# Four more matrix products of a long fp32 kernel by 7 block products in place of 8, with the modulation chunks moved to other stages

## The reference

```python
def conv_ffn(h, w_in, conv_w, conv_b, w_out):
    a = dwconv3(h @ w_in, conv_w, conv_b)
    gate, up = jnp.split(a, 2, axis=-1)
    return (jax.nn.silu(gate) * up) @ w_out
...
    q, k, v, u, g = jnp.split(h_lat @ w_in, splits, axis=-1)      # first mixer
...
    y_lat = jnp.concatenate([a_lat, s_lat], axis=-1) @ w_out      # first mixer
...
    kc = (hc @ w_k).reshape(nb, nl, N_ATTN_HEADS, 2, ATTN_DH)     # differential attention
    k = apply_rope_2(k.reshape(nb, ns, N_ATTN_HEADS, 2, ATTN_DH), cos, sin)
...
    mod = jax.nn.silu(c) @ w_ada[li] + b_ada[li]                  # modulation, all layers
    sh1, sc1, gt1, sh2, sc2, gt2 = jnp.split(mod[:, None, :], 6, axis=-1)
...
    g_a, g_s = jnp.split(jax.nn.sigmoid(gates), 2, axis=-1)
    return (g_a * ya + g_s * ys) @ w_out
```

## Time and profile before

| what | value |
|---|---|
| time, median of 3 runs | 4127.28 us (4125.02 to 4127.33) |
| time of the profiled execution | 4124.42 us |
| its span, first to last instruction | 4122.6 us |
| TensorE busy | 3827.7 us, 93% of the span |
| mean granted TensorE clock | 0.963 of full speed |
| DVE, POOL, ACT busy | 1544.5, 1021.0, 848.5 us |
| DMA traffic | 568.18 MB, mean 138 GB/s |

### The profile page before, as it was taken

One profiled execution on the slowest core, in us unless ns is written; L12 is line 12 of the kernel. 1 busy time (PEld: TensorE's weight loads), 2 busy tenths in 40 slices (PEclk: granted clock), 3 DMA queues, 4 the chain that ended last, 5 costly groups with the idle time before them and its releaser, 6 DMA issues. The chain is left out here.

```text
span 4122.6 us, 40757 instructions
## 1 busy us (share of the span) xinstructions
PE 3827.7 (93%) x14868; PEld 2394.7 (58%) x14868; DVE 1544.5 (37%) x2529; ACT 848.5 (21%) x1794; POOL 1021.0 (25%) x1357
## 2 busy tenths in 40 slices
PE   7998999999999998998989999999989979999994
PEld 3545765555685547667864755756568764444442
DVE  2015465650153334236650434555463351111115
ACT  1106310000031111021010423543420221111111
POOL 0006132210001022104420013300033215555555
PEclk9999999999999999999999999989999979999996
DMA  6610011125311111431222214721112219999995
GB/s 239 223 68 9 31 41 61 61 73 193 137 53 63 36 46 49 152 134 61 92 88 80 77 41 189 311 72 36 41 57 82 71 70 363 390 394 393 378 358 198
DMA packets 132615, 568.18 MB, mean 138 GB/s; under 512 B 20974, under 2 KB 27118, under 8 KB 115840
## 3 DMA queue, kind: packets, MB, share of 16 engines
q0 software_dynamic: 56400, 314.29, 19.2%
q1 hardware_dynamic: 75936, 251.51, 17.6%
q10 hardware_dynamic: 144, 0.52, 0.0%
HBM read 534.58 MB, written 82.84 MB: 150 GB/s over the span
## 5 line engine op out<-in xcount | busy, mean ns | idle before, releaser
L1169 PE MATMUL ps<-arena 128*128 128x384 f32 (+1 forms) x2240 | 610.0, 435 | 13.3 <-DVE arena L1283 10.5
L1169 PEld LDWEIGHTS ps<-arena 128*128 128x128 f32 x2240 | 426.6, 191 | 196.5 <-DVE arena L1283 12.1
L806 PE MATMUL ps<-arena 128*128 128x256 f32 x2088 | 460.8, 381 | 14.7 <-ACT arena L836 10.5
L806 PEld LDWEIGHTS ps<-arena 128*128 128x128 f32 x2088 | 398.1, 191 | 74.8 <-issue 11.2
L3791 PE MATMUL ps<-arena 128*64 128x512 f32 (+1 forms) x1152 | 385.0, 599 | 15.0 <-DMA arena<-w_gate_up,arena 13.2
L636 PE MATMUL ps<-arena 128*128 128x512 f32 (+1 forms) x1072 | 377.9, 510 | 14.5 <-DVEq L4168 8.2
L1386 PE MATMUL ps<-arena 128*128 128x256 f32 x1344 | 299.6, 385 | 24.6 <-DVEq L4168 16.4
L636 PEld LDWEIGHTS ps<-arena 128*128 128x128 f32 x1072 | 202.4, 191 | 196.0 <-issue 160.7
L1386 PEld LDWEIGHTS ps<-arena 128*128 128x128 f32 x1344 | 258.8, 193 | 67.1 <-DVEq L4168 18.8
L3791 PEld LDWEIGHTS ps<-arena 128*64 128x64 f32 (+1 forms) x1152 | 147.6, 164 | 214.5 <-issue 212.0
L1604 PE MATMUL ps<-arena 128*128 128x512 f32 x504 | 222.9, 604 | 11.7 <-DVEq L4168 8.7
(11 more groups left out here) (420 smaller groups left out, 4975.5 us busy)
## 6 DMA issues: line engine op xcount, KB each, us to landing
arena<-ada SPq DMA_DIRECT2D x144, 512.0 KB, 5.2
y_rows<-arena POOLq DMA_DIRECT2D x12, 4096.0 KB, 67.6
arena<-ffn_in SPq DMA_DIRECT2D x88, 512.0 KB, 3.6
arena<-ffn_out SPq DMA_DIRECT2D x32, 512.0 KB, 4.7
arena<-ret_qk SPq DMA_DIRECT2D x16, 512.0 KB, 3.6
arena<-ret_v SPq DMA_DIRECT2D x16, 512.0 KB, 3.4
arena<-ret_g SPq DMA_DIRECT2D x16, 512.0 KB, 4.6
arena<-ret_out SPq DMA_DIRECT2D x16, 512.0 KB, 5.6
```

The costliest lines, as they stand in the source:

```text
L806: mm = pe.matmul(k.ps[:, n % 4, 0:w], lhsT=k.ring[:, u % SLOTS, (c % 8) * P:(c % 8 + 1) * P], rhs=x[:, c, o:o + w], start=c == 0, stop=c = ...
L1169: mm = pe.matmul(k.ps[:, bank, 0:hw], lhsT=a[:, c * P:(c + 1) * P], rhs=b[:, c, :], start=c == 0, stop=c == 3)
```

## The change

Four products go from plain stages to block stages:

- the first mixer's inputs `hyb_qku`, 12 tiles, 768 columns (`CopiedBlocks`, new: ACT copies each finished pair out with scale and function, POOL's block copies come between its sums)
- the first feed-forward output `ffn_out0`, 6 tiles, 22 slices, 768 columns (`PlainBlocks`; its four weight sums lie in unused output tiles, and `restore` gives b12 back at the end)
- the second feed-forward output `ffn_out1`, 6 tiles, 22 slices, 512 columns
- the differential keys `dif_qk`, 8 tiles, 768 columns (`RopeBlocks`, new)

With 22 slices a pair takes three chunks of slices (4, 4 and 3 in each half), and its weights come as 2 times 4 or 2 times 3 blocks for each unit.

The eight modulation sets that follow `Start`'s are placed anew, and `BlockLinear` can now hold chunks: one set in the first mixer's inputs, one in the first mixer's output (`hyb_out`, 3 tiles, now a `ModLinear`, two chunks behind each of the first two tiles), two in the first feed-forward output, two (others than before) in the retention output, and one in each of the two stages of gates. In block stages a set uses bank 7 for its row and for the transposes.

```diff
     def chunk(self, pe, n, u):
         k = self.k
+        if n == 0 and self.bank == self.turn_bank:
+            pe.wait_ge(k.sig("mod_sums_ready").sem, self.made)
...
 class BlockLinear(Stage):
...
     def sync(self, sp):
...
                 sp.dma_start(dst, src).then_inc(k.slot[u % SLOTS], 16)
+            for (i, c), u in zip(self.mods[m], self.mod_u[m]):
+                for j in range(4):
+                    sp.wait_ge(k.sig("unit_used").sem, u + j - SLOTS + 1)
+                    sp.dma_start(k.ring[:, (u + j) % SLOTS, :], self.sets[i].unit(4 * c + j))\
+                        .then_inc(k.slot[(u + j) % SLOTS], 16)
...
             product(self.block(m, 0, 1), h.b21, self.P2).then_inc(k.sig("product_ready").sem, 1)
+            if self.turn_at[m] is not None:
+                self.sets[self.turn_at[m]].turn(pe)
...
             product(self.block(m, 1, 1), h.t4, self.P4).then_inc(k.sig("unit_used").sem, 2)
+            for (i, c), u in zip(self.mods[m], self.mod_u[m]):
+                self.sets[i].chunk(pe, c, u)
             if self.norm is not None and q == self.nc - 1:
                 self.norm.sums(pe, p)
+        if self.turn_at[-1] is not None:
+            self.sets[self.turn_at[-1]].turn(pe)
...
     def scalar(self, act):
...
             self.before(act, p)
+            for m in range(p * self.nc, (p + 1) * self.nc):
+                self.take_rows(act, m)
...
         self.before(act, self.n)
+        self.take_rows(act, self.n * self.nc)
...
     def vector(self, dve):
...
             self.use(dve, p - 1)
+            for m in range(p * self.nc, (p + 1) * self.nc):
+                self.finish_rows(dve, m)
+            self.restore(dve, p, 0)
...
             add(b1, self.P7, a1)
+            self.restore(dve, p, 1)
...
         self.use(dve, self.n - 1)
+        self.finish_rows(dve, self.n * self.nc)
...
+    def restore(self, dve, p, n):
+        k, h = self.k, self.halves
+        if h.t3 is not h.b12 or not h.back or p < self.n - 1:
+            return
+        for q in range(self.nc - 1) if n == 0 else (self.nc - 1,):
+            c0, cn = self.chunks[q]
+            at = slice(c0, c0 + cn)
+            dve.wait_ge(k.sig("product_ready").sem, self.product + 6 * (p * self.nc + q) + 4)
+            dve.tensor_tensor(h.b12[:, at], h.b22[:, at], h.t3[:, at], ALU.subtract)
...
+class CopiedBlocks(BlockLinear):
...
+    def before(self, act, p):
+        k = self.k
+        if p >= 1:
+            act.wait_ge(k.sig("block_added").sem, self.added + 7 * p)
+            for e in range(2):
+                t = 2 * p - 2 + e
+                for s, (o, w) in enumerate(self.spans):
+                    out, src = self.dst[t][:, o:o + w], self.raw[:, (p - 1) % 2, e, o:o + w]
...
+                    a = act.activation(out, src, self.func[t], scale=self.scale[t])
+            a.then_inc(k.sig("pair_finished").sem, 1)
...
+    def meanwhile(self, pool, m):
+        for c in range(2 * m, min(2 * m + 2, KD)):
+            pool.tensor_copy(self.blocked[:, c, :].rearrange("p (b r c) -> p b r c", b=LTT, r=8),
+                             self.k.H[:, c, 0:T].rearrange("p (r b c) -> p b r c", r=8, b=LTT))
...
+class RopeBlocks(PlainBlocks):
...
+    def before(self, act, p):
+        k = self.k
+        if p >= 1:
+            act.wait_ge(k.sig("block_added").sem, self.added + 7 * p)
+            for t in (2 * p - 2, 2 * p - 1):
+                self.rope.turn(act, t, self.dst[:, t, 0:T])
...
+    def use(self, dve, p):
+        if p >= 0:
+            for t in (2 * p, 2 * p + 1):
+                self.rope.apply(dve, t, self.dst[:, t, 0:T], self.dst[:, t, 0:T], self.k.sig("out_taken").sem)
...
-    add(ModLinear(k, d["hyb_qku"], k.H, sets[0][1:3] + sets[1][0:1], (1,) * 10 + (2, 0), tiles(QK) + tiles(U), blocked=HB,
-                  scale=(0.125,) * 4 + (1.0,) * 8, func=(ACT.Copy,) * 8 + (ACT.Gelu_apprx_tanh,) * 4))
+    halves = Halves(k, k.H, 0, N // 2, (F + 6144, F + 6144 + 1536, F + 12288, F + 12288 + 1536), keep=True)
+    add(CopiedBlocks(k, d["hyb_qku"], 12, halves, F + 20480, tiles(QK) + tiles(U), HB, (0.125,) * 4 + (1.0,) * 8,
+                     (ACT.Copy,) * 8 + (ACT.Gelu_apprx_tanh,) * 4, sets=sets[0][1:2], counts=(1, 1, 1, 1, 0, 0)))
...
-    add(Linear(k, d["hyb_out"], 3, k.H, Yo))
+    add(ModLinear(k, d["hyb_out"], k.H, sets[0][2:3], (2, 2, 0), tiles(Yo)[0:3]))
...
-    add(ModLinear(k, d["ffn_out0"], hid, sets[1][1:3] + sets[2][0:1], (1, 1, 1, 0) * 4 + (0, 0), tiles(k.H)[0:6], kt=FT))
+    halves = Halves(k, hid, 0, N // 2, F + FT * N, kt=FT, back=True)
...
+    add(PlainBlocks(k, d["ffn_out0"], 6, halves, sums, k.H, kt=FT, sets=sets[1][0:2], counts=(1,) * 8 + (0,)))
...
-    add(ModLinear(k, d["ret_out"], O, sets[2][1:3], (1,) * 8 + (0, 0),
+    add(ModLinear(k, d["ret_out"], O, sets[1][2:3] + sets[2][0:1], (1,) * 8 + (0, 0),
...
-    add(Linear(k, d["ffn_out1"], 6, hid, k.H, kt=FT, spans=(LAT,)))
+    halves = Halves(k, hid, 0, T // 2, F + FT * N, kt=FT, keep=hid[:, 0:FT // 2, T:N])
+    add(PlainBlocks(k, d["ffn_out1"], 6, halves, F + FT * N + 3 * (FT // 2) * (T // 2), k.H, kt=FT))
...
-    add(RopeLinear(k, d["dif_qk"], K, ((LAT, CTX),) * 8, Rope(k, d, 32, "cos_d", F + 14336, 8), t0=8))
+    add(RopeBlocks(k, d["dif_qk"], 8, Halves(k, k.H, 0, N // 2, F + 16384, keep=True), F + 22528, K,
+                   Rope(k, d, 32, "cos_d", F + 14336, 8), t0=8))
...
-    add(GatedBlocks(k, d["gates"], 8, hidden, F + 24576, YA, YA, ACT.Sigmoid))
+    add(GatedBlocks(k, d["gates"], 8, hidden, F + 24576, YA, YA, ACT.Sigmoid,
+                    sets=sets[2][1:2], counts=(1,) * 4))
...
-    add(GatedBlocks(k, d["gates"], 8, hidden, F + 24576, YS, YS, ACT.Sigmoid, add=YA, t0=8))
+    add(GatedBlocks(k, d["gates"], 8, hidden, F + 24576, YS, YS, ACT.Sigmoid, add=YA, t0=8,
+                    sets=sets[2][2:3], counts=(1,) * 4))
```

More of the change, by code:

```diff
@@ L1066, in __init__ @@
         self.b21, self.b22 = x[:, kh:kt, o:o + hw], x[:, kh:kt, o + hw:o + 2 * hw]
[L1067 to L1068 removed]
+        offs = off if isinstance(off, tuple) else tuple(off + kh * hw * j for j in range(4))
+        self.t1, self.t2, self.t4 = (k.at(o, kh, hw) for o in offs[0:3])
+        if keep is False:
+            self.t3 = self.b12
+        else:
+            self.t3 = k.at(offs[3], kh, hw) if keep is True else keep
         self.chunks = [(c, min(4, kh - c)) for c in range(0, kh, 4)]
@@ L1337, in __init__ @@
         self.nc = nc = len(self.chunks)
-        self.u0 = k.units(2 * self.n * nc)
-        assert self.u0 >= SLOTS
-        k.sig("unit_used").take(2 * self.n * nc)
+        slots = self.n * nc
+        self.sets = sets
+        counts = (0,) * slots if counts is None else counts
+        assert len(counts) == slots and sum(counts) == 4 * len(sets)
+        self.mods = split([(i, c) for i in range(len(sets)) for c in range(4)], counts)
+        self.part_u, self.mod_u, self.turn_at, self.end = [], [], [None] * (slots + 1), [0] * len(sets)
+        for m, mods in enumerate(self.mods):
+            self.part_u.append(k.units(2))
+            self.mod_u.append([k.units(4) for _ in mods])
+            for (i, c), u in zip(mods, self.mod_u[m]):
+                sets[i].bank = sets[i].turn_bank = 7
+                if c == 3:
+                    self.end[i] = u + 4
+                    self.turn_at[m + 1] = i
+        assert self.part_u[0] >= SLOTS
+        k.sig("unit_used").take(2 * slots + 16 * len(sets))
         self.product = k.sig("product_ready").take(6 * self.n * nc)
@@ L1344, in __init__ @@
         self.added = k.sig("block_added").take(7 * self.n)
-        self.sums = [k.at(off + 512 * j, 512) for j in range(4)]
+        self.sums = off if isinstance(off, list) else [k.at(off + 512 * j, 512) for j in range(4)]
     def source(self, t, q):
-        return self.w[t + self.t0], UC
+        if self.kt == KD:
+            return self.w[t + self.t0], UC
+        c0, cn = self.chunks[q]
+        return self.w[t].rearrange("p (h x) -> p h x", h=2)[:, :, c0 * P:(c0 + cn) * P], 2 * cn * P
     def out(self, p):
@@ L1445, in gpsimd, with meanwhile, take_rows @@
             pool.tensor_tensor(s4[:, 0:w], a12, s2[:, 0:w], ALU.subtract).then_inc(k.sig("weights_summed").sem, 1)
+            self.meanwhile(pool, m)
+    def meanwhile(self, pool, m): pass
+    def take_rows(self, act, m):
+        if self.turn_at[m] is not None:
+            self.sets[self.turn_at[m]].take(act, self.end[self.turn_at[m]])
     def before(self, act, p): pass
@@ L1459, in scalar, with finish_rows, restore @@
         self.before(act, self.n)
+        self.take_rows(act, self.n * self.nc)
+    def finish_rows(self, dve, m):
+        if self.turn_at[m] is not None:
+            self.sets[self.turn_at[m]].finish(dve)
+    def restore(self, dve, p, n): pass
     def use(self, dve, p): pass
```

48 lines of the change are left out of this document (35 added, 13 removed).

## The result

The changed kernel takes 4071.62 us (median of 4 runs, 4066.28 to 4076.24) against 4126.41 for the kernel before on the same chips; the ratio is 0.9867, with a 95% interval from 0.985 to 0.9884. The forecast was 4074 in a range from 4062 to 4098, and "faster". The profiled execution's span went from 4122.6 to 4066.9 us, by 55.7.

What follows compares the result with a forecast made beforehand. TensorE, busy in 93% of the span, was taken as the bound: matmul time plus stage ends. Terms -31.9 + 13.2 - 30.0 - 12.7 - 7.6 + 16.0 = -53.0 took 4127.28 to 4074 us, range 4062 to 4098.

Steps and rivals of the forecast that it cites:

- Price of a matmul by its width: Matmul time goes by columns: 0.3231 us an instruction at width 384, 0.2175 at 256; 7 products for 8 save 1/8.
- Price of a chunk: Each modulation chunk behind a tile costs TensorE 1.93 us, wherever it is put.
- The rival in which 20 chunks starve: Each of 20 chunks in block stages holds TensorE for 3.8 us, 76 us in all, total 4150; chance 0.04.
- First mixer's inputs: Stage of `hyb_qku`: 155.2 us becomes 119.9, its end +2.4, cold clock +1; together -31.9 us.
- the 1 of 0 to 3: Cold clock after the gap of about 3 us ending the first mixer's inputs: +1 us taken, from 0 to 3.
- First mixer's output: Stage of `hyb_out`: four chunks, two sets of load waits and a turn, +13.5 us, end 0.3 shorter: +13.2.
- the bound of +18: Upper bound in us for the first mixer's output, if each load wait doubles.
- Feed-forward outputs and keys: First feed-forward output -30.0 us, second feed-forward output -12.7, differential keys -7.6.
- The cover of the subtractions: In the first feed-forward output, last products hide three DVE subtractions giving b12 back: 0 us taken, 7 without cover.
- Gates: Each of two gate stages takes 4 chunks, the fourth after the last product: +8.6 and +7.4, together +16.0 us.
- The rivals of dearer and cheaper ends: Block stages' ends and starts cost 26 us more, total 4100, chance 0.15; or ends cost 8 less, 4066, chance 0.13.
- The sum: All stage terms together: -53.0 us, from the median 4127.28 to 4074.3, so 4074.

Runs made afterwards that it cites:

- Three undone parts: The changed kernel with plain tiles again in the first mixer's inputs (4081.34 us), the first feed-forward output (4090.56), or the second and the keys (4088.64).

## Why the prediction was right

**Price of a matmul by its width.** It held. The pair of tiles at 916.69 in the timeline after takes 18.35 us for 56 instructions, and the whole stage at 2097.75, cold start and all, 102.67 for 462. Three undone parts gave 13.2, 21.1 and 21.9 us back against 14, 21.7 and 20.6 expected. So 7 products for 8 saved what columns say.

**Price of a chunk.** It held for single chunks in every kind of stage, and no chunk waited in a block stage with one a slot. The rival in which 20 chunks starve came up nowhere. It had a true core: as soon as two chunks share a slot, TensorE waits 2.8 to 3.2 us.

**First mixer's inputs.** 123.09 for 122.9, and 1 of cold clock was put behind it. In this profile the gap of 3.08 us at its end was not followed by half clock, the next stage's piece took 41.47 us as before. But in five of the nine profiles with this gap it was, at 1.5 to 1.7 us, so the 1 of 0 to 3 was right on average, and its 0 here is luck.

**First mixer's output.** This is the term that was sized least well, +14.7 for +13.2. The refills were where they had been put, with waits of 1.89, 0.64 and 2.34 us for 2 x (1.86 + 0.77). What was missing is the clock: after the second wait a chunk took 2.51 us for 1.90 and a tile 11.63 for 10.59, 1.6 us in all. It stays inside the bound of +18.

**Feed-forward outputs and keys.** Off by 0.7, 0.5 and 0.2 us. The cover of the subtractions is shown by moving them away; the wait for a weight sum at the keys' start is 0.28 us for 0.2. In the keys two misses cancel. No cold clock came: 16 instructions took 5.43 us behind 2.94 us of idle time, at a granted clock of 1.00, where 2.93 us had been followed by 0.50 before. Against these 0.9 us stand an end 0.4 longer, and products that took 0.326 us an instruction and not 0.323, 0.6 more.

**Gates.** Off by 0.3 and 0.2 us. The 6.2 us from the last product to the next stage were 5.7 (3066.19, where the last chunk starts, to 3071.87).

**The rivals of dearer and cheaper ends.** Neither came as a whole; of the cheaper one, only gaps that stayed warm did, here behind the mixer's inputs and behind the second gates. DVE and POOL work against each other at stage starts as in the earlier trace rows, but TensorE waited for neither in the mixer's inputs and 0.28 us in the keys.

**The sum.** Each large term is within 1.5 us. The span fell by 55.7 us and not by 53.0: the listed stages gave 0.6 less than forecast, and stages that had been counted at nothing gave 3.3 more. Of these the 4.9 behind the second gates came, to within 1 us, in every profile with the set's turn there; the rest is what profiles differ by. That the total agrees within 3 us rests on both, and on the cold clocks that failed to come, and is partly luck; the seven stages agree one by one.

## What to carry to other kernels

Where TensorE is busy without gaps, a change of its work can be forecast from three prices read from the same kernel: time by column, what follows the last product of a stage, and what a refill of the load ring costs. A ring has a rhythm: work that takes half of it in one piece is free when single pieces alternate with other work, and costs the latency of a load less the first piece's own time when two follow each other (here waits of 1.9 to 3.2 us, 2.6 to 5.9 with what the clock lost), however long the work ahead was, since the load can't be ordered before that work frees its slots. What the clock does behind an idle gap of about 3 us can't be forecast for one run; count it at its mean. Put such pieces first in a stage, where the ring is full.

## What was not expected

**The set's turn keeps the clock up.** The stage behind the second gates took 16.21 us before and 14.75 after. Before, TensorE had been idle for 4.64 us; now the set's transposes come between, its idle pieces are 2.48 and 0.81 us, and the granted clock of the stage behind is 1.00. With the chunks moved forward the gap of 4.64 and the 16.35 us are back. So 1.5 us of the gates' +15.5 are given back by the neighbour, which the forecast did not count.

**A later stretch goes with it.** The stretch from there to the router's last part took 137.8 us before and 134.4 after. The windows over the first 5 us of the router's matmuls, for the changed kernel and then for the one with the gates' chunks forward:

```profile
3281.40:3286.40 5.00, 5.00 (x35) 5.00 (x35) 0.00 (x0) 0.00 (x0) 1.19 (x2) 0.76 0.01 5
```

```profile
3295.58:3300.58 5.00, 5.00 (x24) 5.00 (x24) 0.00 (x0) 0.00 (x0) 1.26 (x2) 0.50 0.02 6
```

The granted clock is 0.76 in one and 0.50 in the other, after the same wait of 2.8 us for `w_router`. The three kernels with a cold start behind the gates took 137.8, 137.8 and 138.2 us for this stretch, and the ten without took 133.9 to 135.2. That the two go together is a reading of thirteen profiles; why is open.

**The same gap, two outcomes.** Other stages that no kernel here changes also differ in steps of 1.7 us. The first token product after the mixer's inputs, behind the same gap of 3.08 us, took 42.19 in the changed kernel's first profile and 43.88 in its second:

```profile
171.87 43.16 PE L1034 MATMUL ps<-arena 128*128 128x512 f32 x96 [3.08 <-POOLq L4302]
```

The granted clock over its first 5 us was 1.00 in the first profile and 0.66 in the second. By the Trainium skill (TensorE: Matmul & The Clock Gate, Part 1: The HAM clock gate) half clock is the default, activity releases it, and the number of cold matmuls varies from run to run. These two profiles agree with it. It does not explain the router's stretch, which came out alike in all profiles with the same end of the gates about 100 us before.
